# Expert tiles in native fp32, two products side by side, and late tiles loaded by a flag

## The reference

```python
def hier_moe(h, w_group, b_group, w_expert, b_expert, w_gate, w_up, w_down):
    ...
    top_p, top_i = lax.top_k(e_prob, TOP_K_EXPERTS)          # 2 of the 8 experts of the token's group
    ...
    for e in range(N_EXPERTS):                               # 32 experts, 1024 -> 512 -> 1024
        hid = jax.nn.silu(t @ w_gate[e]) * (t @ w_up[e])
        out = out + combine[:, e:e + 1] * (hid @ w_down[e])
```

## Time and profile before

| | |
|---|---|
| median of 3 runs | 2270.79 us (2269.74 to 2271.43) |
| span of the profiled execution | 2268.9 us (its own time has no other record; the medians stand 1.9 us above the span) |
| mean granted clock of PE | 0.986 |
| busy: PE, DVE, ACT, POOL | 97%, 69%, 52%, 4% |
| DMA | 496.88 MB, 219 GB/s over the span |

### The profile page before, as it was taken

One profiled execution on the slowest core, in us unless ns is written; L12 is line 12 of the kernel. 1 busy time (PEld: TensorE's weight loads), 2 busy tenths in 40 slices (PEclk: granted clock), 3 DMA queues, 4 the chain that ended last, 5 costly groups with the idle time before them and its releaser, 6 DMA issues.

```text
span 2268.9 us, 26611 instructions
## 1 busy us (share of the span) xinstructions
PE 2194.2 (97%) x9804; PEld 1610.6 (71%) x9804; DVE 1573.7 (69%) x1576; ACT 1168.7 (52%) x1185; POOL 90.1 (4%) x79
## 2 busy tenths in 40 slices
PE   7989996999999999999999999999999999999999
PEld 5435765655665665565888887888888888878887
DVE  6989558888888878886555883855465558756554
ACT  4124524676666666665433585553354346665332
POOL 2750000000000000000000000000000000000000
PEclk9989997999999999999999999999999999999999
DMA  6224343999999999995555543555455544435653
GB/s 235 93 75 135 108 178 134 353 371 361 358 364 365 369 361 363 366 367 217 194 195 167 172 159 117 204 186 171 164 192 197 195 159 162 155 130 169 205 183 112
DMA packets 166451, 496.88 MB, mean 219 GB/s; under 512 B 10272, under 2 KB 21792, under 8 KB 136400
## 3 DMA queue, kind: packets, MB, share of 16 engines
q1 hardware_dynamic: 164528, 491.70, 60.8%
q10 hardware_dynamic: 1616, 3.24, 0.4%
q0 software_dynamic: 208, 0.59, 0.1%
HBM read 494.45 MB, written 1.05 MB: 218 GB/s over the span
## 4 chain that ended last, share of the span: by engine, by line
PE 82%; DVE 11%; issue 3%; ACT 3%; POOL 0%; DMA 0%; DVEq 0%; ACTq 0%; POOLq 0%
PE ps L1025 20%; PE ps L1035 15%; PE ps L1034 15%; PE ps L1511 9%; PE ps L1492 5%; PE ps L1496 5%; PE ps L1193 3%; PE ps L1480 2%; PE ps L1549 1%; DVE W_r L2859 1%; DVE xn L2582 1%; PE ps L1161 1%; PE ps L1162 1%; DVE W L2587 1%; ACT w_hi L2051 1%
## 5 line engine op out<-in xcount | busy, mean ns | idle before, releaser
L2398 DVE TENSOR_TENSOR w_lo<-raw,w_hi 128x2048 fp32r<-128x2048 f32 (+2 forms) x153 | 336.1, 2208 | 136.6 <-ACT w_hi L1830 129.4
L1830 ACT ACTIVATE w_hi<-raw 128x2048 fp32r<-128x2048 f32 (+2 forms) x153 | 281.6, 1849 | 227.3 <-PE ps L1025 194.1
L1035 PE MATMUL ps<-w_hi,a_lo 128*128 128x512 f32 (+1 forms) x984 | 371.6, 378 | 0.0
L1025 PE MATMUL ps<-w_hi,a_hi 128*128 128x512 f32 (+1 forms) x936 | 356.9, 381 | 0.2 <-DVEq L2438 0.2
L1034 PE MATMUL ps<-w_lo,a_hi 128*128 128x512 f32 (+1 forms) x928 | 349.5, 377 | 0.0
L1035 PEld LDWEIGHTS ps<-w_hi,a_lo 128*128 128x128 f32 x984 | 185.2, 188 | 34.6
L1025 PEld LDWEIGHTS ps<-w_hi,a_hi 128*128 128x128 f32 x936 | 176.2, 188 | 33.1 <-issue 2.1
L1034 PEld LDWEIGHTS ps<-w_lo,a_hi 128*128 128x128 f32 x928 | 174.8, 188 | 30.8
L1492 PE MATMUL ps<-w_hi,W_r 128*128 128x512 f32 x468 | 189.5, 405 | 4.3 <-DVE raw_r L2859 3.4
L2398 DVE TENSOR_TENSOR y_lo<-raw,y_hi 128x2048 fp32r<-128x2048 f32 x51 | 116.9, 2291 | 51.2 <-ACT y_hi L1830 48.6
L1830 ACT ACTIVATE y_hi<-raw 128x2048 fp32r<-128x2048 f32 x51 | 97.8, 1917 | 72.7 <-PE ps L1025 63.1
(11 more groups left out here) (468 smaller groups left out, 4325.5 us busy)
## 6 DMA issues: line engine op xcount, KB each, us to landing
raw<-in_w_in SPq DMA_DIRECT2D x56, 1024.0 KB, 5.1
raw<-in_ffn_w_gate SPq DMA_DIRECT2D x44, 1024.0 KB, 5.1
raw<-in_ffn_w_up SPq DMA_DIRECT2D x44, 1024.0 KB, 5.1
raw<-in_ffn_w_down SPq DMA_DIRECT2D x40, 1024.0 KB, 6.2
raw<-in_w_up SPq DMA_DIRECT2D x30, 1024.0 KB, 8.2
raw<-in_w_gate SPq DMA_DIRECT2D x30, 1024.0 KB, 7.2
lo_f<-in_w_up SPq DMA_DIRECT2D x30, 1024.0 KB, 8.1
lo_f<-in_w_down SPq DMA_DIRECT2D x29, 1024.0 KB, 7.9
```

The costliest lines, as they stand in the source:

```text
L1025: return released(pe.matmul(dst, a, b, skip_group_check=True, **kw))
L1035: return pe.matmul(dst, a_l, b_h, start=False, stop=final, skip_group_check=True)
L1830: act.activation(E.hi_view(name, ahead), E.raw_view(name, ahead), ACT.Copy).then_inc(hi_split, 1)
L2398: tt(E.lo_view(name, ahead), E.raw_view(name, ahead), E.hi_view(name, ahead).bitcast(F32), ALU.subtract)\
```

## The change

- The rows of a tile are no longer split: `packed_rows` holds plain fp32, 64 columns. The hi and lo parts of gathered rows are added up in PSUM by the gather itself.
- Gate and up of the next tile become one step, `expert_gate_up`: for each of the 8 blocks and each of gate and up, two native fp32 products of 64 stationary columns by 256 columns, one on each half of the array's columns (`tile_position=(0, 0)` and `(0, 64)`). The first gives columns 0 to 255 of the result in partitions 0 to 63, the second columns 256 to 511 in partitions 64 to 127 of the same bank. Gate and up share a bank. `expert_down` is paired in the same way.
- `expert_rounded`, `expert_lower`, `lower_half` and `halves_added` go; ACT makes the silu and DVE the product from PSUM, 128 x 256.
- `spread` and `out_parts` have two buffers, and the output of a tile is added to the sums two tiles later (`scatter_before`). POOL clears them with six memsets, since the first two additions have nothing yet.
- `ex_i` has 7 flags more: 1 where the late tile has rows. SP reads them and gives each late load as `cond`.
- `final_period` is an ordinary period followed by the last two additions; the residual waits for both halves of the output.

```diff
-MOE_RAW, MOE_HI = 8, 4
+MOE_RAW = 8
...
-            def load_expert(name, half, e, ahead=None):
+            def load_expert(name, half, e, ahead=None, cond=None):
...
-                sp.dma_start(E.expert_raw((name, half))[0], src).then_inc(
+                sp.dma_start(E.expert_raw((name, half)), src, cond=cond).then_inc(
                     expert_loaded[n0 % MOE_RAW], 16)
...
+            late_used = [sp.value_load(ex_i[0:1, 8 + j:9 + j], min_val=0, max_val=1) for j in range(EXTRA_TILES)]
...
             for k in periods("tail"):
-                load_period(k, lambda q: late_expert[q])
+                load_period(k, lambda q: late_expert[q], used_of=lambda q: late_used[q])
```

```diff
+            def expert_gate_up(k, name, group, q):
+
+                dst = bank(name)
+                for i, kind in enumerate("gu"):
+                    for half in range(2):
+                        w = landed(((kind, k), half))
+                        for j in range(4):
+                            a = packed_rows[group][:, 4 * half + j, q, :]
+                            for side, rows in enumerate((lower_rows, upper_rows)):
+                                at = 512 * j + SEQ * side
+                                m = pe.matmul(dst[rows, SEQ * i:SEQ * i + SEQ], a, w[:, at:at + SEQ],
+                                              start=i == half == j == 0, stop=i == half == 1 and j == 3,
+                                              skip_group_check=True, tile_position=(0, SLOTS * side))
+                        if (kind, half) != ("u", 1):
+                            m.then_inc(expert_used, 1)
+                fill(m, name)
+
+            def expert_down(k, releases):
+
+                dst = bank(("y", k))
                 for half in range(2):
+                    w = landed((("d", k), half))
+                    for r in range(2):
+                        for c, rows in enumerate((lower_rows, upper_rows)):
+                            at = r * D + c * 512
+                            m = pe.matmul(dst[rows], hidT[:, r, half, :], w[:, at:at + 512], start=half == r == 0,
+                                          stop=half == r == 1, skip_group_check=True, tile_position=(0, SLOTS * c))
+                            if releases and half == r == c == 0:
+                                m.then_inc(expert_used, 1)
...
             def period(k, acc):
                 which, q = k
+                turn_expert(k)
+                if has_gather(k):
+                    i = (q + 1) % GROUP_TILES
+                    if i == 0 and which == "loop":
                         pe.wait_ge(done["picked"], nth("picked", (which, q - 1)))
+                    gather(("G", k), i)
+                scatter_before(k, acc)
+                if has_next(k):
+                    if (q + 1) % GROUP_TILES == 0:
+                        pe.wait_ge(done["gathered_act"], nth("gathered_act", (which, q - 1)))
+                    expert_gate_up(k, ("gu", k), (q + 1) // GROUP_TILES % 2, (q + 1) % GROUP_TILES)
                 pe.wait_ge(done["expert_turned"], nth("expert_turned", k))
+                expert_down(k, releases=has_next(k))
...
+                k, before_it = final_tile, ("tail", EXTRA_TILES - 2)
+                period(k, acc)
+                scatter(nth("spread", before_it), lambda c: nth("out_split", (before_it, c)), acc, before_it[1] % 2)
```

```diff
@@ ACT, period
-                if up:
-                    lower_half((k, "g"), bank_of[("g", "first")], E.gate_fill(k), low_g)
-                if gathers:
-                    gathered_copy(("G", k, 0), kb, group)
-                if gate:
-                    expert_rounded(("g", k), 0)
-                    expert_rounded(("g", k), 1)
...
+                if has_gather(k):
+                    gathered_copy(("G", k), k, (q + 1) % GROUP_TILES, ((q + 1) // GROUP_TILES + 1) % 2)
+                if has_next(k):
+                    gated(k, ("gu", k))
+                act.wait_ge(done["scattered"], nth("scattered", k))
+                act.wait_ge(bank_filled[bank_of[("y", k)]], fills(("y", k)))
                 output_rounded(k, 0)
                 output_rounded(k, 1)
@@ DVE, late_experts and period
+                ts(ex_f[:, 8:16], ex_f[:, 0:8], EXPERTS - 0.5, None, ALU.is_lt).then_inc(vector_step, 1)
...
-                if gate:
-                    expert_lower(("g", k), 0)
-                    expert_lower(("g", k), 1)
-                if up:
-                    halves_added((k, "u"), bank_of[("u", k)], fills(("u", k)), low_u)
-                    hidden_rows(k, column(tile + 1))
...
+                if which == "loop" and q % GROUP_TILES == 2:
+                    picked(k, column(regs["moe"] * 2 + (q // GROUP_TILES + 2)))
+                if has_next(k):
+                    hidden_rows(k, ("gu", k), column(tile + 1))
...
+                if k == final_tile:
+                    residual(lambda c, t: ("moe", "acc", c, t), "moe", parts=(0,))
@@ DVE, before the loop (experts, route)
-                dve.memset(hid_e[SLOTS:P], 0.0).then_inc(vector_step, 1)
...
-                expert_lower(("u", "first"), 0)
-                expert_lower(("u", "first"), 1)
...
-                expert_lower(("g", "second"), 0)
@@ POOL
+            pool.wait_ge(done["rows"], nth("rows", ("m", 1, 1)))
+            for q in range(2):
+                pool.memset(spread[q].bitcast(F32), 0.0).then_inc(zeroed, 1)
+                for c in range(2):
+                    pool.memset(out_parts[q][:, c, :].bitcast(F32), 0.0).then_inc(zeroed, 1)
```

More of the change, by code:

```diff
@@ L361, in plan @@
     fill("ranks", 6); fill("token_rows", 7); fill("slot_weights", 6)
[L362 to L374, removed]
+    for i in range(KB // 2):
+        fill(("G", "first", 0, i), i)
+        mark("gathered_act" if i % 2 else "gathered", ("first", 0, i))
+    expert_unit(("g", "first")); expert_unit(("u", "first"))
+    fill(("gu", "first"), 0)
+    fill(("G", "first", 1), 3)
+    mark("gathered_act", ("first", 1))
+    mark("gated", "first"); mark("expert_hidden", "first")
+    mark("spread", ("none", 0), ("none", 1))
+    mark("out_split", *(("none", q, c) for q in range(2) for c in range(2)))
     for c in range(2):
@@ L869, in bass_hybrid_moe_then_swa_gla, with has_next, has_gather @@
         stretch1 = straight(("u", 0), (("wo", 1), 1))
-        FIRST_TILES = [("g", "first"), ("u", "first"), ("g", "second")]
-        def period_units(k):
+        def has_next(k):
             which, q = k
-            up, gate = which == "loop" or q < EXTRA_TILES - 1, which == "loop" or q < EXTRA_TILES - 2
-            return [("u", k)] * up + [("d", k)] + [("g", k)] * gate
-        def next_units(k):
+            return which == "loop" or q < EXTRA_TILES - 1
+        def has_gather(k):
             which, q = k
[L879 to L889, removed]
+            return which == "loop" or q < GROUP_TILES - 1
         def periods(which):
@@ new lines, in scatter @@
+            def scatter(spread_value, split_value, acc, parity, columns=range(2)):
+                pe.wait_ge(done["spread"], spread_value)
+                for c in columns:
+                    pe.wait_ge(done["out_split"], split_value(c))
+                    for t in range(2):
+                        m = pe.matmul(acc[t][c], spread[parity][:, t * P:t * P + P], out_parts[parity][:, c, :], start=False,
+                                      stop=False, skip_group_check=True)
+                return m
@@ L1520, in period, with scatter_before @@
+            def scatter_before(k, acc):
+                scatter(marks["spread"].number(k, regs) - 1,
+                        lambda c: marks["out_split"].number((k, c), regs) - 3, acc, k[1] % 2).then_inc(done["scattered"], 1)
             def period(k, acc):
                 which, q = k
-                up, gate = which == "loop" or q < EXTRA_TILES - 1, which == "loop" or q < EXTRA_TILES - 2
-                gathers = which == "loop" or q < GROUP_TILES - 1
-                pe.wait_ge(done["expert_hidden"], marks["expert_hidden"].number(k, regs) if up
-                           else nth("expert_hidden", ("tail", EXTRA_TILES - 2)))
```

430 lines of the change are left out of this document (139 added, 291 removed).

## The result

The changed kernel takes 2146.93 us (median of 4 runs, 2145.72 to 2149.12) against 2270.26 us (4 runs of the kernel before): a ratio of 0.9457, 95% interval 0.9444 to 0.947, 123 us or 5.4% less. The forecast was 2142. The profiled execution has a span of 2143.9 us.

A forecast was written before the change was run, and what follows sets the result against it. PE bounds the expert stage before, the DMA's loads after: loop to 846, late tiles 72.9, final tile 14.3 give 933 against 1062.56, 129 us less: profile 2140, median 2142 us. Range 2126 to 2156, chance 0.66.

The forecast's parts named there:

- A pair costs one product: Gate/up and down on PE: the second product of a pair is free; gate/up 6.9 us, down 3.4.
- Loads at 415 GB/s: Expert loop: with a deep queue the DMA takes 2.53 us a load, 15.2 a tile, above PE's 12.6.
- rival 1: Expert loop: loads run at 379 GB/s as on average before, +43 us, 2185; chance 0.15.
- rival 5: Expert loop: a memory ceiling keeps the sustained rate at 364 GB/s, 2206 us; chance 0.04.
- Start of the loop at 385: Start of the expert stage: the loop begins at 385 us, 13 us earlier, bounds 8 and 15.
- The loop's end: Expert loop: last load at 844 us, tile 31's down ends at 846 against 951.6, -105.6 us.
- Late tiles: After the loop: 42 loads vanish, tiles run at PE's pace, 72.9 us against 96.6.
- rival 4: Late tiles: the flags don't stop the transfers, 42 more loads, 2168 us; chance 0.04.
- Final tile: End of the expert stage: about 14.3 us again, bounds 12 and 17.
- Rival 2: Gate/up and down: pairs run one after the other, period 23.0 us, PE the bound, 2482 us; chance 0.04.
- Rival 3: PE's clock in the loop: idle pieces lower it to a mean of 0.75, +50 us, 2192; chance 0.05.
- SP waiting for PE in the loop: Expert loop: SP still waiting for PE was named as a sign that the prediction is wrong; no size given.

The follow-up runs named there:

- e9: Changed kernel with the products of both sides on the lower 64 columns, into the same rows of the bank: 2494.04 us.
- e11: Changed kernel with half-size loads in the loop and PE's loop written out as straight code: 2091.91 us.
- e6: Changed kernel without the products on the upper 64 columns, in gate/up and down: 2146.47 us.
- e5: Changed kernel with SP allowed four loads ahead of PE instead of eight: 2207.89 us.
- e5b: Changed kernel with SP allowed only two loads ahead of PE: 2539.18 us.
- e7: Changed kernel with four edits of order at the loop's start, the final tile and the next stage's weights: 2149.34 us.
- e8: Changed kernel with each tile's gather made twice, eight more matmuls a tile: 2163.80 us.
- e4: Changed kernel with loads of half the size in the loop, PE's work as it is: 2113.27 us.
- e2: Changed kernel with, within each load, all products of the lower 64 columns first, then all of the upper 64: 2170.87 us.
- e1: Changed kernel with the flags taken off, so the 42 loads of the seven late tiles are always made: 2174.76 us.

## Why the prediction was right, step by step

- **PE is the bound before, and the halves make room for the DMA to become it: right.** e9 and e11 bound it from both sides: with the halves not used a tile takes 23.14 us, with loads of half the size 12.8, and as it is 14.9.
- **A pair costs one product: right**, 1.0 (e6), from one row of a lone pair. Sixteen pairs take 6.96 us (6.9), down 3.53 (3.4), a late tile 12.8 (12.6) and 11.86 (11.7). The 2 us more a tile, if weight loads didn't overlap on shared rows, don't show: passes follow every (842.08 - 838.57) / 16 = 0.219 us.
- **Loads at 415 GB/s: right in kind, 422 measured**, 2.485 us a load instead of 2.527, sustained over all of 480 to 800 us. So rival 1 (379), rival 5 (364) and the Trainium skill's limit for a core (about 358 GB/s; DMA: Bandwidth & Descriptors, Specifications) are out for this core. The reason that I gave, the deep queue, is borne out by e5 and e5b.
- **Start of the loop at 385: 382.66 in this profile, in part luck.** The router's first matmul stands at 357.03 us here, at 360.64 in the kernel before and between 357.6 and 360.9 in the experiments, whose loops start at 383.3 to 386.2 (e9, with its longer gate/up, aside). 3.6 of the 15.3 us are from ahead of the stage, and the profiled execution is the fastest of the four.
- **The loop's end: the step that failed, hidden by another.** I had the last load land at 844 and tile 31's down end 2 us behind it, 846. It landed near 837 (306 GB/s from 830 to 840), 7 earlier, and tile 32 began at 849.06, 12 behind it: in a period the gate/up of the *next* tile stands before the down of this one, and that of tile 32 is computed though its loads are skipped. I left it out, a path of 10 us. The two errors leave +3, and that they offset each other is luck: with the measured rate and the same path left out the forecast would have been 2135, 12 us off instead of 5.
- **Late tiles: right** (74.0 against 72.9, 3 GB/s). A skipped load holds SP for 0.07 to 0.09 us, a real one for 0.33. The flags are worth 24 to 28 us, rival 4's 26.
- **Final tile: right**, 14.6 against 14.3; e7 shows where 2.85 of it was (the bank of the outputs before, and DVE's second subtraction).
- **Rival 2 (2482)** would have been the result without the halves: e9, 2494. **Rival 3 (the clock)** is out as I had it: with gaps of under 1 us the granted clock stays at 1.00. But around the jump's gaps of 4 to 4.6 us it falls to 0.50, and I had no rival for a stall of instructions: it costs 11 us in e8 and 20 in e4, kernels close to this one, and could have taken a tenth of the gain.
- **A sign that was wrong.** I wrote that SP waiting for PE in the loop would speak against me. It still does, 273 of 350 us in three rows of the waits from 450 to 800 (138.4 in 71 waits the longest). So the sign was badly chosen, and the result doesn't answer to it: with all eight buffers handed out, SP's next issue is released by PE, whoever is the bound. What tells is the DMA's share and PE's own waits for loads.

## What to carry to other kernels

When the engine that is the bound gets faster, look for the next bound: here PE could go from 17.3 to 12.8 us a tile, and the loads stopped it at 14.9. Look also at what the order of work leaves to be done behind the last transfer. Two products on the two halves of the columns cost one in pairs, and 10% more a tile in blocks of two or four. A transfer-bound loop needs its queue kept deep (here more than four loads of 1 MB). Look at a long loop's jumps back in each profile: here one cost PE up to 12.5 us or nothing, and writing the loop out took the stalls away but gained nothing on a kernel without them.

## What the runs showed of the hardware

- **Instructions of a loop are sometimes fetched again at the jump back.** Three jumps each: three stalls in e2, e4 and e8, two in e1, e5 and e7, none in the changed kernel, in e6, in e5b and in the kernel before. In e9 there are instruction packets at all three jumps, but its periods there are only 0.3 to 1.6 us longer. These are one profiled execution of each. The changed kernel and e1 (and e4, e5) have the same instructions on PE, so the length alone doesn't decide; what does is open, and so is what sets the length of a stall: e4, with the DMA at share 0.70, still loses 5.8 to 7.5 us a jump. The Trainium skill (Runtime: NRT & Kernel Launch, Instruction fetch mechanics) says that PE's instruction memory is refilled in blocks of 16 KiB and that a taken branch out of the window forces a fetch. The packets of 16 KB and the stalls agree; the jumps without a stall and with one such packet or none near them don't follow from it.
- **The clock was halved around two long gaps.** In e8 PE stood 4.58 us before 502.04 and 3.94 before 507.32. The granted clock is 0.72 from 500 to 504, 0.50 from 504 to 512 and 1.00 from 512 on, with PE busy from 507.3. In the changed kernel, with gaps of 0.3 to 0.7 us, three a tile, it is 1.00 from 480 to 800.
- **DMA at 422 GB/s on one core for 430 us** (400 to 830), and 241 when SP may be only two loads ahead.
